# The last layer norm of a decoder step: one engine's work spread over three, the short tile moved up, and the adding transfers reordered

## The chip, the cores and the metric

The kernel runs on one core of a Trainium2 chip. The metric is the device time of one execution in microseconds (us). Three executions of the kernel before took 1103.56, 1101.90 and 1106.04 us; the median is 1103.56 us. The trace that is read here is of one further execution.

## What is computed

The kernel is one inference step of a two-layer decoder trunk for a prompt of 512 tokens and a sample group of 8 tokens, 1024 features each, in float32. Each sub-layer ends in a layer norm. The change concerns only the very last one, the norm behind the mixture of experts of layer 1:

```python
def layer_norm(x, g, b):
    mu = jnp.mean(xf, axis=-1, keepdims=True)
    var = jnp.mean(jnp.square(xf - mu), axis=-1, keepdims=True)
    return ((xf - mu) * lax.rsqrt(var + LN_EPS) * g + b)
...
        xp = layer_norm(ALPHA * xp + hier_moe(xp, ...), ln_g[l, 2], ln_b[l, 2])
        xs = layer_norm(ALPHA * xs + hier_moe(xs, ...), ln_g[l, 2], ln_b[l, 2])
    return (xp, xs, ...)
```

hier_moe gives every token to two experts, its first and its second choice. The token's row of x, already scaled by ALPHA, gets both experts' output rows added, and is then normed and stored.

## The kernel before

The 520 tokens lie in five row tiles, `ROWS = [128, 128, 128, 128, 8]`: tiles 0 to 3 are the prompt, tile 4 is the sample group. `x[:, t, :]` holds a tile, one token per partition, 1024 floats long.

The experts work on sorted blocks of 128 token slots. A block's output goes through ScalarE (L2220) into `ybuf`. All but the last two blocks of layer 1 are written by an indirect transfer from GpSimd's queue (L838) into `y_tok[1]`, a DRAM buffer of 2 x 520 rows: the first half for the tokens' first choices, the second half for the second choices. The last two blocks are held back in SBUF.

The end of the kernel, on each engine:

- GpSimd (POOL) waits until all scattered blocks are in DRAM and then issues ten adding transfers, `add_rows(t, c)` (L871), which read `y_tok` and add onto `x[:, t, :]`; c is the choice. Two adds onto one tile must not overlap, so `add_rows(t, 1)` waits on the queue until `add_rows(t, 0)` has landed (`added[t]`). The order is (0,0) (1,0) (0,1) (2,0) (1,1) (3,0) (2,1) (4,0) (3,1) (4,1). Behind them it loads the count of overflowing blocks, branches past code for such blocks (there are none), and does nothing more.
- TensorE (PE) multiplies the two held blocks by one-hot rows, `held_blocks` (L1666, and L1670 for the short tile), tile by tile, into one of four PSUM pairs, key `("cmb", t)`. A full tile has four matmuls in the code (two blocks, two halves of the row), which the trace records as eight.
- VectorE (DVE), `combine_last`: `summed(t)` waits for both adds of the tile and for its PSUM pair, adds PSUM onto x with the row sum as a by-product (L2773; for tile 4 four pieces at L2778 and a reduce at L2782), and makes minus the mean (L2723). `rooted(t)` waits for ScalarE's square root, takes the reciprocal (L2759), forms (x - mean) * g in place (L2762) and then * scale + b in place (L2763). The order is summed(0), summed(1), rooted(0), summed(2), rooted(1), and so on, so one tile's statistics are taken while the tile before it is finished.
- ScalarE (ACT): `row_squares` sums the squares of x - mean (L1957), a Sqrt activation follows (L2354), and ScalarE's queue issues the stores of the finished tiles (L2348), two tiles behind.

g and b of this norm lie in `lnb[:, 0, :]` and `lnb[:, 1, :]`, one row on every partition. All tiles go in the order 0, 1, 2, 3, 4. xT, which the changed kernel takes as scratch space, has held weights of the last experts' blocks and is read for the last time by the matmuls before `held_blocks`.

Of the kernel before, what the change touches and what calls it, by code (L numbers as in the profile page):

```python
# [27 lines left out]
P = 128  # L28
# [139 lines left out]
def keys(text):  # L168

    return [tuple(int(w) if w.isdigit() else w for w in word.split(".")) for word in text.split()]  # L170
# [67 lines left out]

LATENT_GROUPS = [slice(0, P), slice(P, 2 * P), slice(2 * P, 3 * P), slice(3 * P, 416)]
LATENT_ROWS = {2: [0], 3: [1], 4: [2, 3, 4]}  # L240
COMBINE_DVE = keys("""a.0 b.0 a.1 s.0 b.1 n.0 a.2 s.1 x.0 r.0 b.2 n.1 a.3 s.2 x.1 r.1 b.3 n.2 a.4 s.3 x.2 r.2 b.4 n.3 s.4 x.3 r.3 n.4 x.4 r.4""")


def psum_jobs():

    jobs = []
    jobs += [("xT", -1, t) for t in range(NT)]
    jobs += [("qa", j) for j in range(4)] + [("ka", 0), ("ka", 1), ("va",)]
    jobs += [("kaTok",), ("qr", 0)]
    for step, i in sliding_steps(len(SWA_BLOCKS)):  # L250
        jobs += SWA_WEAVE[i] if step == "W" else [("swa" + step, i)]
    jobs += SWA_SAMPLE
    for n in range(4):
        jobs += [("retS", n), ("retK", n)] + RET_WEAVE.get(("K", n), [])
        jobs += [("retO", n), ("retU", n)] + RET_WEAVE.get(("U", n), [])
        if n:
            jobs += [("retG", n - 1)]
    for l in range(DEPTH):
        if l == 1:
            jobs += LATENT_PE  # L260
            jobs += [("qn", j) for j in (2, 3)]
            jobs += [("qrope", 0)]
            jobs += [("ql", h) for h in range(8)]
            for t in range(NT):
                jobs += ([("qrope", t)] if t else []) + ([("qrT", t - 1)] if t else [])
            jobs += [("qrT", 4)]
            jobs += [("mla" + s, i) for s, i in latent_steps(len(MLA_BLOCKS))]
            jobs += [("pkT", 0), ("pkT", 1), ("pN",)] + [key for key in PAGE_PE if key[0] != "row"]
            jobs += [("uv", j) for j in range(4)]
        jobs += [memory_job(l, *key) for key in MEM_PE[l] if key[0] != "ms2"]  # L270
        if l == 0:
            jobs += [("memF", 1, 0), ("memF", 1, 1), ("rank", 0), ("mkv", 1, 0), ("table", 0), ("mkv", 1, 1)]
        else:
            jobs += [("rank", 1), ("table", 1)]
        for s, b in block_order():
            jobs += [("moe" + s, l, b)] + ([("mkT", 1)] if (l, s, b) == (0, "H", 0) else [])
    jobs += [("cmb", t) for t in range(NT)]
    return jobs


def decoder_step(nc, io, outs):
# [83 lines left out]
    with ExitStack() as ctx:  # L365
# [49 lines left out]
        def part(*dims, at0=None):  # L415
# [7 lines left out]
            if len(dims) > 1:  # L423
# [87 lines left out]
        assert at[0] <= ARENA - EXTRA_SLOTS * PIECE  # L511
        y_front = part(3, 2, D, at0=4096)
        y_of = [y_front[:, t] for t in range(3)] + [pbuf, pT]
        spill_rows, spill_hot = xs[:, 1, :], xsT[:, 1, :, :].rearrange("p k n -> p (k n)")

        at[0] = 0
# [36 lines left out]
                 "var_ready", "rstd_ready", "x_ready", "last_ready", "swapped", "rope_done", "negmax_ready", "probs_ready",  # L553
                 "vec_step", "pool_step", "g_exp", "qd_ready", "vm_ready", "q_state_zero", "q_state_ready", "gated_ready",
                 "row_neg", "row_exp", "row_probs", "router_neg", "router_exp", "moe_exp",
                 "moe_done", "picks_ready", "places_ready", "route_in", "rope_in", "sum_ready", "squares_ready", "lnc_in", "cleared", "held_ready", "root_ready",
                 "wr_zero", "stores_out", "rows_out",
                 "x_out", "x_stored", "half_hidden", "q_wide_zero", "q_wide_ready", "states_out", "tokens_ready", "sq_done", "qrS_zero", "oin_ready", "qrtok_ready"]
        s = {n: sem(n) for n in names}
# [109 lines left out]
        def _(sp):  # L669
# [105 lines left out]
                    expert_rows(0)  # L775
            spilled_weights(1, len(W))


        @block.gpsimd
        def _(pool):  # L780
# [43 lines left out]
            def dispatch(l):  # L824
# [42 lines left out]
                def add_rows(t, c):  # L867
                    first = c * T + t * P
                    if c:
                        pool.wait_ge(added[t], 16)  # L870
                    pool.dma_start(x[0:ROWS[t], t, :], y_tok[1][first:first + ROWS[t], :], accum_op=ALU.add).then_inc(added[t], 16)  # L871

                if l:
                    for i in range(2):
                        pool.wait_ge(y_out[i], 16 * sum(SCATTERED) // 2)
                    add_rows(0, 0)
                    for t in range(NT):
                        if t + 1 < NT:
                            add_rows(t + 1, 0)
                        add_rows(t, 1)  # L880
                sem_ = spill_s[l]
                with spilled(pool, l):
                    full(pool, ("moeX", l, BLOCKS_M - 1))
# [91 lines left out]
            for l in range(DEPTH):  # L975
# [15 lines left out]
                if l == 0:  # L991
                    for t in range(NT):
                        tile_power(t)
                        if t == 3:
                            power(rms[0:P, 0, 2:4])
                    for t in range(1, NT):
                        power(rms[0:ROWS[t], t % 2, 2:4])
                    pool.wait_ge(s["stored"], 16 * n_stored[0])
                    pool.nop().then_inc(s["moe_done"], 1)
            pool.wait_ge(s["stored"], 16 * n_stored[0])  # L1000


        @block.tensor
        def _(pe):
# [649 lines left out]
            def held_blocks():  # L1654

                pe.wait_ge(s["held_ready"], 2)
                for t in range(NT):
                    key = ("cmb", t)
                    o = open_(key)
                    r = ROWS[t]  # L1660
# [260 lines left out]
        def _(act):  # L1921
# [27 lines left out]

            take_xT(-1)  # L1950

            def row_squares(i, t):

                r = ROWS[t]
                act.wait_ge(s["sum_ready"], NT * (i // 3) + t + 1)
                unread = pbuf[0:r, t % 2, :] if i == 3 * DEPTH - 1 else y_of[t][0:r, 0, :]
                act.activation(unread, x[0:r, t, :], ACT.Square, bias=centre[0:r, t % 3:t % 3 + 1],  # L1957
                               accum_out=squares[0:r, t % 3:t % 3 + 1]).then_inc(s["squares_ready"], 1)

            def take_memory(key):  # L1960
                if key[0] == "memF":
# [283 lines left out]
            def latent_attention():  # L2245
# [29 lines left out]
                def turned(i, t):  # L2275
                    take_xT(i, range(t, t + 1))
                    if t + 2 < NT:
                        row_squares(i, t + 2)

                for t in range(2):  # L2280
                    row_squares(2, t)
                steps = {"xT": turned, "oin": latent_squares, "oinT": back,
                         "ukT": lambda: take(("ukT",), ukT, lambda o: o[:, 0:512].rearrange("p (c q) -> p c q", c=4))}
                for key in LATENT_IN:
# [57 lines left out]
            memory_stage(1)  # L2342
            experts(1)

            def store_rows(t):
                act.wait_ge(s["last_ready"], t + 1)
                dst = y_prompt[0, t * P:t * P + P] if t < 4 else y_sample.rearrange("b s d -> (b s) d")
                act.dma_start(dst, x[0:ROWS[t], t, :]).then_inc(s["x_stored"], 16)  # L2348

            for t in range(NT):  # L2350
                row_squares(3 * DEPTH - 1, t)
                r = ROWS[t]
                act.wait_ge(s["squares_ready"], NT + t + 1)
                act.activation(rstd[0:r, t, 0:1], squares[0:r, t % 3:t % 3 + 1], ACT.Sqrt, scale=1.0 / D,  # L2354
                               bias=small[0:r, EPSILON:EPSILON + 1]).then_inc(s["root_ready"], 1)
                if t >= 2:
                    store_rows(t - 2)
            for t in range(NT - 2, NT):
                store_rows(t)
            act.wait_ge(s["x_stored"], 16 * NT)  # L2360


        @block.vector
        def _(dve):
# [354 lines left out]
                dve.wait_ge(y_in[t][0], 16 * (i // 3 + 1))  # L2719
                link(dve.tensor_tensor(x[0:r, t, :], x[0:r, t, :], y_of[t][0:r, 0, :], ALU.add))  # L2720

            def mean_of(i, t, total):
                dve.tensor_scalar(centre[0:ROWS[t], t % 3:t % 3 + 1], total, -1.0 / D, None, ALU.mult).then_inc(s["sum_ready"], 1)  # L2723

            def second_add(i, t):
                r = ROWS[t]
                total = sums[0:r, t % 3:t % 3 + 1]
                dve.wait_ge(y_in[t][1], 16 * (i // 3 + 1))
                link(dve.scalar_tensor_tensor(x[0:r, t, :], y_of[t][0:r, 1, :], 1.0, x[0:r, t, :], ALU.mult, ALU.add, accum_out=total))
                mean_of(i, t, total)  # L2730

            def combine_latents(after):

# [17 lines left out]

            def combine_last():

                def rooted(t):
                    r = ROWS[t]
                    xt = x[0:r, t, :]
                    scale, mid = rstd[0:r, t, 0:1], centre[0:r, t % 3:t % 3 + 1]
                    dve.wait_ge(s["root_ready"], t + 1)
                    link(dve.reciprocal(scale, scale))  # L2759
                    if t == 0:  # L2760
                        dve.wait_ge(s["ln_in"], 32 * 6)
                    link(dve.scalar_tensor_tensor(xt, xt, mid, lnb[0:r, 0, :], ALU.add, ALU.mult))  # L2762
                    dve.scalar_tensor_tensor(xt, xt, scale, lnb[0:r, 1, :], ALU.mult, ALU.add).then_inc(s["last_ready"], 1)  # L2763

                def summed(t):
                    r = ROWS[t]
                    xt = x[0:r, t, :]
                    total = sums[0:r, t % 3:t % 3 + 1]
                    key = ("cmb", t)
                    dve.wait_ge(added[t], 32)  # L2770
                    full(dve, key)
# [3 lines left out]
                    else:  # L2775
# [4 lines left out]
                        free(ins, key)  # L2780
                        taken(dve, key)
                        link(dve.tensor_reduce(total, rowmax[0:r, 0, :], AX.X, ALU.add))  # L2782
                    mean_of(5, t, total)

                summed(0)
                for t in range(NT):
                    if t + 1 < NT:
                        summed(t + 1)
                    rooted(t)

            def first_max(out, m, v, tmp):

# [348 lines left out]
```

## Time and profile before

| | us |
|---|---|
| median of three executions | 1103.56 |
| lowest, highest | 1101.90, 1106.04 |
| span of the profiled execution | 1105.1 |
| TensorE busy | 989.1 |
| VectorE busy | 524.0 |
| ScalarE busy | 353.4 |
| GpSimd busy | 253.4 |

The span is counted from the first instruction, and all times of the trace are positions in it. PE is busy for 90% of it, but not at its end: it does nothing after 1090.1 us, and the last 15 us belong to the other engines and the transfers. A "timeline" lists instructions with their start and length and, in brackets, how long the engine had idled before and what ended that. A "chain" is followed back from the last instruction through whatever released each step. "Windows" give, for a stretch, the busy time of each engine, the granted TensorE clock as a share of full speed, the mean busy share of the 16 DMA engines and the rate in GB/s.

### The profile page before, as it was taken

To read this page: it belongs to the slowest core of one execution; us is meant where nothing else is said; L and a number is where in the kernel's file an instruction comes from. 1 tells how busy PE (TensorE), PEld (TensorE's weight loads), DVE (VectorE), ACT (ScalarE), POOL (GpSimd) and SP (SyncE) were. 2 spreads that over 40 slices of the span, in tenths; PEclk is the share of its full clock that TensorE was granted. 3 is DMA by queue.
4 is the path that set the end of the run, shared out by engine and by line. 5 is a ranking of instruction groups with operands and counts; after the bars stand their busy time and mean duration, and the time that the engine had idled before them with its cause. 6 is when DMAs were issued, how large, how long until landed. Compare 5 with 4: busy or idle time off the path is not lost.

```text
span 1105.1 us, 17827 instructions
## 1 busy us (share of the span) xinstructions
PE 989.1 (90%) x6978; PEld 617.2 (56%) x6978; DVE 524.0 (47%) x1102; ACT 353.4 (32%) x879; POOL 253.4 (23%) x281
## 2 busy tenths in 40 slices
PE   7998999989989998899998398998999946999994
PEld 6886788887446766533332256657568633333331
DVE  0226520566657657143322654773187571334227
ACT  2335531110011523233432342554115422333423
POOL 2224400051500001536311126300000014362121
PEclk9999999998989987899999698899899956999998
DMA  9434702052205407789997404331434063999976
GB/s 313 91 93 114 232 6 77 5 188 77 67 16 179 192 38 300 271 324 410 404 420 273 176 8 101 79 132 40 136 146 185 31 230 102 337 397 405 418 217 161
DMA packets 81594, 204.17 MB, mean 185 GB/s; under 512 B 22682, under 2 KB 47938, under 8 KB 72288
## 3 DMA queue, kind: packets, MB, share of 16 engines
q1 hardware_dynamic: 60976, 151.83, 37.4%
q0 software_dynamic: 19936, 48.99, 14.4%
q10 hardware_dynamic: 592, 2.13, 0.5%
q8 instruction: 59, 0.97, 0.4%
q14 instruction: 31, 0.25, 0.1%
HBM read 184.92 MB, written 25.92 MB: 191 GB/s over the span
## 4 chain that ended last, share of the span: by engine, by line
PE 75%; DVE 13%; DMA 4%; ACT 4%; issue 3%; POOL 0%; SPq 0%; POOLq 0%; DVEq 0%; ACTq 0%
PE PS L1556 15%; PE PS L1393 10%; PE PS L1035 9%; PE PS L1132 6%; PE PS L1571 6%; PE PS L1416 3%; ACT arena L1923 2%; PE PS L1097 2%; DMA x<-y_tok 2%; PE PS L1023 2%; PE PS L1767 2%; PE PS L1058 2%; PE PS L1777 2%; PE PS L1692 2%; PE PS L1545 2%
## 5 line engine op out<-in xcount | busy, mean ns | idle before, releaser
L1923 ACT ACTIVATE arena<-PS 32x520 f32<-32x520 f32 (+10 forms) x150 | 75.1, 513 | 194.2 <-PE PS L1035 47.3
L1556 PE MATMUL PS<-ring,arena 128*32 128x512 f32 x648 | 116.9, 592 | 1.4 <-DVE arena L2934 1.4
L1556 PE MATMUL PS<-arena 128*32 128x512 f32 x648 | 112.8, 614 | 3.5 <-issue 2.6
L1035 PE MATMUL PS<-xT,ring 128*128 128x260 f32 x448 | 102.2, 389 | 4.1 <-DVE arena L2380 3.1
L1035 PEld LDWEIGHTS PS<-xT,ring 128*128 128x128 f32 x448 | 85.5, 192 | 19.8 <-DVE arena L2380 5.1
L2950 DVE COPY arena<-PS 128x256 f32<-128x256 f32 x24 | 10.2, 424 | 171.2 <-PE PS L1564 171.2
L2194 ACT ACTIVATE arena<-PS,lnc 128x128 f32<-128x128 f32 x192 | 69.5, 473 | 42.8 <-PE PS L1545 42.8
L800 POOL TENSOR_TENSOR rstd<-rstd,small 128x1 f32<-128x1 f32 (+1 forms) x25 | 16.3, 651 | 272.7 <-DVE rstd L2668 245.3
L1571 PE MATMUL PS<-ring,arena 128*32 128x512 f32 x432 | 69.0, 595 | 1.2 <-DVE arena L2950 1.2
L1023 PE MATMUL PS<-ident,x 128*128 128x128 f32 (+1 forms) x240 | 39.4, 319 | 33.0 <-DVE x L2744 20.3
L1132 PE MATMUL PS<-ring,xT 128*128 128x256 f32 (+2 forms) x336 | 66.8, 361 | 0.0
L1556 PEld LDWEIGHTS PS<-arena 128*32 128x32 f32 x648 | 30.9, 113 | 62.3 <-issue 58.3
L1132 PEld LDWEIGHTS PS<-ring,xT 128*128 128x128 f32 (+1 forms) x336 | 58.2, 189 | 7.5
L838 POOL DMA_INDIRECT y_tok<-arena,slot_dest x22 | 22.3, 1012 | 174.1 <-ACT arena L2220 168.3
L1023 PEld LDWEIGHTS PS<-ident,x 128*128 128x128 f32 (+1 forms) x240 | 35.1, 202 | 42.0 <-issue 33.2
L1556 PEld LDWEIGHTS PS<-ring,arena 128*32 128x32 f32 x648 | 31.2, 110 | 47.3 <-issue 43.1
L1393 PE MATMUL PS<-ring,xT 128*128 128x512 f32 x128 | 56.8, 593 | 0.7 <-ACT xT L1923 0.7
L1932 ACT ACTIVATE xT<-PS,lnc 128x128 f32<-128x128 f32 (+1 forms) x100 | 37.6, 437 | 54.8 <-PE PS L1023 35.6
L2212 ACT ACTIVATE arena<-PS 128x256 f32<-128x256 f32 x24 | 9.2, 385 | 143.1 <-PE PS L1556 143.1
L1556 PE MATMUL PS<-xT,arena 128*32 128x512 f32 x240 | 50.3, 593 | 0.8 <-DVE arena L2934 0.8
L1393 PE MATMUL PS<-ring,arena 128*128 128x512 f32 x96 | 48.4, 645 | 2.1 <-issue 2.1
L2030 ACT ACTIVATE pbuf<-PS,negmax 128x256 f32<-128x256 f32 (+3 forms) x96 | 45.0, 480 | 10.1 <-DVE negmax L2427 10.0
(422 smaller groups left out, 1858.3 us busy)
## 6 DMA issues: line engine op xcount, KB each, us to landing
arena<-in_moe_w_in_dram SPq DMA_DIRECT2D x27, 1024.0 KB, 10.1
ring<-in_moe_w_in_dram SPq DMA_DIRECT2D x27, 1024.0 KB, 13.5
ring<-in_moe_w_out_dram SPq DMA_DIRECT2D x18, 1024.0 KB, 12.3
ring<-in_w_in_even_dram SPq DMA_DIRECT2D x10, 1024.0 KB, 11.7
xT<-in_moe_w_in_dram SPq DMA_DIRECT2D x10, 1024.0 KB, 13.4
arena<-in_moe_w_out_dram SPq DMA_DIRECT2D x8, 1024.0 KB, 14.5
xT<-in_moe_w_out_dram SPq DMA_DIRECT2D x6, 1024.0 KB, 15.5
y_tok<-in_c_zeros_dram POOLq DMA_DIRECT2D x8, 512.0 KB, 10.2
```

Source lines behind the costliest of these rows:

```text
L838: pool.indirect_dma_start(y_tok[l][:, :], bass.IndirectOffsetOnAxis(ap=slot_dest[:, b:b + 1], axis=0), ybuf[:, buf, :], None, bounds_check ...
L1023: mm = pe.transpose(o[:, chunk_cols(k, r)], by_k[:, k, :], ident[0:r, 0:r])
L1035: mm = pe.matmul(o[out_rows, 512 * h:512 * h + HALF], lhs(k), rhs(k)[:, HALF * h:HALF * h + HALF], start=(k == 0), stop=(k == nk - 1))
L1132: mm = pe.matmul(o[0:ROWS[t], n * width:n * width + width], xT[:, k, tile_cols(t)], w[:, k, cols], start=(k == 0), stop=(k == KD - 1))
L1393: mm = pe.matmul(o[0:ROWS[t], 512 * h:512 * h + 512], out_part(i, 2 * n + k, t), w[:, k, 512 * h:512 * h + 512], start=(n == 0 and k == 0) ...
L1416: mm = pe.matmul(o[:, j * r:j * r + r], w[:, k, j * P:j * P + P], xT[:, k, tile_cols(t)], start=(k == 0), stop=(k == KD - 1))
L1556: mm = pe.matmul(o[group(q), 0:512], xT_[:, k, group(q)], w(q, k), start=(k == 0), stop=(k == KD - 1), **quarter(q))
L1571: mm = pe.matmul(o[group(q), 512 * h:512 * h + 512], a[:, c, group(q)], w(q)[:, c, 512 * h:512 * h + 512], start=(c == 0), stop=(c == 1), ...
L1923: return act.activation(dst, src, ACT.Copy)
L1932: ins = act.activation(dst(k), src(k), ACT.Identity, scale=lnc[:, i, 0, k:k + 1], bias=lnc[:, i, 1, k:k + 1])
L2030: ins = act.activation(prob_view(kind, i)[:, h, :], score_view(kind, i)[:, h, :], ACT.Exp, bias=negmax[:, n % 2, h:h + 1], scale=SCALE[kin ...
L2194: ins = act.activation(dst[:, k, :], o[:, k * P:k * P + P], ACT.Identity, scale=lnc[:, 3 * l + 1, 0, k:k + 1], bias=lnc[:, 3 * l + 1, 1, k ...
```

## The change

The last norm is done in the tile order 0, 4, 1, 2, 3 on all engines. Its element work is split. For each tile VectorE adds PSUM, makes the mean and at once forms (x - mean) * g, not into x but into a scratch row (`centred_rows`, four in xT and one in pT). ScalarE, beside squares and root, multiplies that row by the reciprocal root and writes it to x (`scaled`). GpSimd adds b in place. Only the last tile (3) is finished on VectorE, scale and b in one instruction (`finished`). The stores go from SyncE's queue instead of ScalarE's, one for each tile in the tile order. The ten adding transfers are issued as (0,0) (4,0) (1,0) (2,0) (0,1) (4,1) (3,0) (1,1) (2,1) (3,1).

```diff
+LAST_TILES = [0, 4, 1, 2, 3]
+LAST_ADDS = [(0, 0), (4, 0), (1, 0), (2, 0), (0, 1), (4, 1), (3, 0), (1, 1), (2, 1), (3, 1)]
...
-    jobs += [("cmb", t) for t in range(NT)]
+    jobs += [("cmb", t) for t in LAST_TILES]
...
+        centred_rows = [xT[:, :, :].rearrange("p k n -> p (k n)")[:, D * i:D * i + D] for i in range(4)] + [pT[:, 0, :]]
...
+            for n, t in enumerate(LAST_TILES):
+
+                if n < NT - 1:
+                    sp.wait_ge(s["last_ready"], n + 1)
+                else:
+                    sp.wait_ge(s["end_ready"], 1)
+                dst = y_prompt[0, t * P:t * P + P] if t < 4 else y_sample.rearrange("b s d -> (b s) d")
+                sp.dma_start(dst, x[0:ROWS[t], t, :]).then_inc(s["x_stored"], 16)
...
-                    add_rows(0, 0)
-                    for t in range(NT):
-                        if t + 1 < NT:
-                            add_rows(t + 1, 0)
-                        add_rows(t, 1)
+                    for t, c in LAST_ADDS:
+                        add_rows(t, c)
...
+            pool.wait_ge(s["ln_in"], 32 * 6)
+            for n, t in enumerate(LAST_TILES[:-1]):
+
+                r = ROWS[t]
+                pool.wait_ge(s["scaled_ready"], n + 1)
+                pool.tensor_tensor(x[0:r, t, :], x[0:r, t, :], lnb[0:r, 1, :], ALU.add).then_inc(s["last_ready"], 1)
...
-                for t in range(NT):
+                for t in LAST_TILES:
                     key = ("cmb", t)
...
+            def scaled(n):
+
+                t = LAST_TILES[n]
                 r = ROWS[t]
-                act.wait_ge(s["squares_ready"], NT + t + 1)
-                act.activation(rstd[0:r, t, 0:1], squares[0:r, t % 3:t % 3 + 1], ACT.Sqrt, scale=1.0 / D,
+                act.wait_ge(s["centred_ready"], n + 1)
+                act.wait_ge(s["inverse_ready"], n + 1)
+                act.activation(x[0:r, t, :], centred_rows[n][0:r, :], ACT.Copy, scale=rstd[0:r, t, 0:1]).then_inc(s["scaled_ready"], 1)
+
+            for n, t in enumerate(LAST_TILES):
+                row_squares(3 * DEPTH - 1, n, t)
+                r = ROWS[t]
+                act.wait_ge(s["squares_ready"], NT + n + 1)
+                act.activation(rstd[0:r, t, 0:1], squares[0:r, n % 3:n % 3 + 1], ACT.Sqrt, scale=1.0 / D,
                                bias=small[0:r, EPSILON:EPSILON + 1]).then_inc(s["root_ready"], 1)
-                if t >= 2:
-                    store_rows(t - 2)
-            for t in range(NT - 2, NT):
-                store_rows(t)
-            act.wait_ge(s["x_stored"], 16 * NT)
+                if n:
+                    scaled(n - 1)
...
+                def finished(n, t):
+
+                    r = ROWS[t]
+                    dve.wait_ge(s["inverse_ready"], NT)
+                    dve.wait_ge(s["centred_ready"], NT)
+                    dve.scalar_tensor_tensor(x[0:r, t, :], centred_rows[n][0:r, :], rstd[0:r, t, 0:1], lnb[0:r, 1, :], ALU.mult, ALU.add
+                                             ).then_inc(s["end_ready"], 1)
...
+                    mean_of(n, t, total)
+                    dve.wait_ge(s["sum_ready"], NT + n + 1)
+                    if n == 0:
+                        dve.wait_ge(s["ln_in"], 32 * 6)
+                    dve.scalar_tensor_tensor(centred_rows[n][0:r, :], xt, centre[0:r, n % 3:n % 3 + 1], lnb[0:r, 0, :], ALU.add, ALU.mult
+                                             ).then_inc(s["centred_ready"], 1)
+
+                for n, t in enumerate(LAST_TILES):
+                    summed(n, t)
+                    if n:
+                        rooted(n - 1, LAST_TILES[n - 1])
+                rooted(NT - 1, LAST_TILES[-1])
+                finished(NT - 1, LAST_TILES[-1])
```

`rooted(n, t)` now holds only the wait for the root and the reciprocal. n is the position in the order, t the tile.

## Rows read from the trace of the kernel before

**Rows 1.** Chain of waits towards the end: start us, us, what.

```profile
1064.87 5.49 DMA x<-y_tok
...
1071.28 8.46 DMA x<-y_tok
...
1080.02 7.22 DMA x<-y_tok
```

**Rows 2.** Windows: us, each engine's busy time, TensorE clock, DMA share, GB/s.

```profile
1073.00:1085.00 12.00, 12.00 (x43) 4.93 (x36) 3.99 (x8) 5.14 (x7) 3.46 (x4) 1.00 1.05 202
...
1101.00:1102.00 1.00, 0.00 (x0) 0.00 (x0) 0.96 (x2) 0.00 (x0) 0.00 (x0) 0.50 0.96 389
```

**Rows 3.** Timeline of VectorE, the tail: start us, us, engine, line, tiles, shapes.

```profile
1078.89 1.23 DVE L2773 SCALAR_TENSOR_TENSOR x<-PS,x 128x1024 f32<-128x1024 f32 x1 [7.53 <-PE PS L1666]
...
1087.26 1.23 DVE L2773 SCALAR_TENSOR_TENSOR x<-PS,x 128x1024 f32<-128x1024 f32 x1 [0.80 <-DMA x<-y_tok]
...
1088.53 0.15 DVE L2723 TENSOR_SCALAR bns<-bns 128x1 f32<-128x1 f32 x1
...
1088.79 1.29 DVE L2762 SCALAR_TENSOR_TENSOR x<-x,bns,lnb 128x1024 f32<-128x1024 f32 x1
...
1091.31 1.22 DVE L2773 SCALAR_TENSOR_TENSOR x<-PS,x 128x1024 f32<-128x1024 f32 x1
...
1095.36 0.41 DVE L2778 SCALAR_TENSOR_TENSOR x<-PS,x 8x256 f32<-8x256 f32 x1
...
1097.31 0.14 DVE L2723 TENSOR_SCALAR bns<-bns 8x1 f32<-8x1 f32 x1
...
1101.56 1.27 DVE L2763 SCALAR_TENSOR_TENSOR x<-x,rstd,lnb 8x1024 f32<-8x1024 f32 x1
```

**Rows 4.** TensorE's lines of the held blocks: ns min/median/max, first and last start.

```profile
L1666 PE MATMUL PS<-arena x32: 590/592/697, 1075.1 to 1088.5; 128*128 128x512 f32 x32
...
L1670 PE MATMUL PS<-arena x16: 377/379/383, 1089.0 to 1089.7; 128*8 128x256 f32 x16
```

**Rows 5.** Timeline and one line of ScalarE, the tail, with its stores.

```profile
1075.26 1.11 ACT L2220 ACTIVATE arena<-PS,arena 128x1024 f32<-128x1024 f32 x1 [3.50 <-PE PS L1571]
...
1088.72 1.15 ACT L1957 ACTIVATE pbuf<-x,bns 128x1024 f32<-128x1024 f32 x1 [3.37 <-DVE bns L2723]
...
1089.99 0.29 ACT L2354 ACTIVATE rstd<-bns,small 128x1 f32<-128x1 f32 x1
...
L2348 ACTq DMA_DIRECT2D out_dram<-x x5: 338/339/540, 1090.0 to 1102.9; - x5
```

**Rows 6.** GpSimd's additions of b in earlier norms, by line: ns min/median/max.

```profile
L816 POOL TENSOR_TENSOR x<-x,lnb x10: 2360/2372/2380, 468.8 to 993.5; 128x1024 f32<-128x1024 f32 x8, 8x1024 f32<-8x1024 f32 x2
```

**Rows 7.** Timeline near 982 us, and the same VectorE line over the whole span.

```profile
982.41 2.37 POOL L816 TENSOR_TENSOR x<-x,lnb 128x1024 f32<-128x1024 f32 x1
982.62 2.31 DVE L2931 TENSOR_SCALAR arena<-arena 128x256 f32<-128x256 f32 x1
...
L2931 DVE TENSOR_SCALAR arena<-arena x24: 282/286/2307, 470.7 to 1066.7; 128x256 f32<-128x256 f32 x24
```

**Rows 8.** Timeline from 281 us: VectorE beside four additions of GpSimd.

```profile
281.30 8.05 POOL L961 TENSOR_TENSOR arena<-arena,small 8x1024 f32<-8x1024 f32 x4
281.99 1.47 DVE L2395 TENSOR_TENSOR arena<-xT,arena 8x256 f32<-8x256 f32 x1
...
287.17 0.41 DVE L2395 TENSOR_TENSOR arena<-xT,arena 8x256 f32<-8x256 f32 x1
287.62 1.22 DVE L2659 SCALAR_TENSOR_TENSOR x<-x,PS 128x1024 f32<-128x1024 f32 x1
```

**Rows 9.** Timeline near 619 us, and GpSimd's line L800 over the whole span.

```profile
618.87 1.22 DVE L2729 SCALAR_TENSOR_TENSOR x<-arena,x 128x1024 f32<-128x1024 f32 x1
619.04 1.48 POOL L800 TENSOR_TENSOR rstd<-rstd,small 128x1 f32<-128x1 f32 x1 [10.81 <-DVE rstd L2739]
...
L800 POOL TENSOR_TENSOR rstd<-rstd,small x25: 536/550/1480, 290.7 to 889.8; 128x1 f32<-128x1 f32 x20, 8x1 f32<-8x1 f32 x5
```

## What the change is expected to do

> **What bounds the kernel now.** I read the chain of waits towards the end first, then the tail's timeline engine by engine, then the windows. Up to 1087 us the chain runs through the adding transfers: the one at 1064.87 lands 5.49 us later, at 1070.36, that at 1071.28 lands at 1079.74, that at 1080.02 at 1087.24 [rows 1]. Between 1073 and 1085 us the DMA engines are at a share of 1.05 and move 202 GB/s [rows 2], so a 512 KB add costs 2.5 us of them, and TensorE is busy throughout the same 12 us. VectorE waits for TensorE before tile 0 (at 1078.89) and for a transfer before tile 2 (1087.26, after only 0.80 us idle) [rows 3]. From there it never waits: tile 2 to tile 3 takes 1091.31 - 1087.26 = 4.05 us, and its last instruction ends at 1101.56 + 1.27 = 1102.8 [rows 3]. The last store is issued at 1102.9 [rows 5]; the span is 1105.1. So the end belongs to VectorE from 1087 us, to transfers and TensorE before. TensorE's last matmul of the held blocks starts at 1089.7 [rows 4], so tile 3 can't be combined before 1090.1 whatever else is done.
>
> **The adds in another order.** The bytes are the same, 8 x 512 KB and 2 x 32 KB. Now four adds without a wait among them stand in the queue, and (0,1), (4,1), (3,0), (1,1) follow while data still flows. Each waits for a first add that was issued three or more places earlier, so I expect no gap in the flow. Tile 4's two adds are early; tile 3's second is last. But (0,1), third in the queue before, now stands behind (2,0): it takes the place of the fourth large transfer, which landed at 1079.74 [rows 1]. Tile 0 therefore starts between 1078.9 (TensorE, as before [rows 3]) and 1079.9; I take 1079.3, 0.4 later than before. The other tiles follow at 2.5 us each: tile 1 after about 84.4, tile 2 after 86.9, tile 3 after 89.4 at the latest (1000 left out here and below). VectorE comes later than that to each of them (below). On TensorE the short tile's matmuls move from the end to second place, a microsecond, and tile 3's end stays at 90.1.
>
> **VectorE.** A full tile is now the add (1.27 us to the mean), 0.19 from the mean to the next dependent instruction (that is what ScalarE's start at 88.72 is behind 88.53 [rows 3, 5]), one long instruction instead of two, 1.25 (the two before took 91.31 - 88.79 = 2.52), and 0.07 for the reciprocal's issue (88.79 - 88.53 less 0.19): 2.78 us in place of 4.05 [rows 3]. The short tile takes 97.31 - 95.36 = 1.95 for its pieces, so 3.46. Undisturbed: tile 0 at 79.3, short tile at 82.0, reciprocal of tile 0 at 85.4, tile 1 at 85.47, its centred product 86.93 to 88.2.
>
> **ScalarE.** Squares to root is 89.99 - 88.72 = 1.27, the root 0.29; the scaling is one ACTIVATE, 1.11 for the same form at L2220 and 1.15 at L1957 [rows 5]; I take 1.13. Together 2.7 us in each 2.78: it fits, and the load of the root's table lies where it lay.
>
> **GpSimd.** It adds b to four tiles, the short one at full price since the free length counts: 2.37 us each, from ten instructions between 2.36 and 2.38 [rows 6], 9.5 us in all against 7 us taken off VectorE at 1.28 a piece. It is free for this from about 85 us, behind its last transfer.
>
> **The shared resource.** Alone GpSimd would keep pace. But the rows show that it and VectorE exclude each other. A VectorE TENSOR_SCALAR that takes 0.29 us took 2.31 when GpSimd's L816 had begun 0.21 before it, and ended 0.15 after GpSimd (982.62 + 2.31 against 982.41 + 2.37) [rows 7]. A TENSOR_TENSOR with both inputs in SBUF took 1.47 in place of 0.41 beside GpSimd's L961; beside the same line an add of PSUM and SBUF took its usual 1.22 [rows 8]. The other way round GpSimd's power took 1.48 instead of 0.55 when VectorE's SCALAR_TENSOR_TENSOR of two SBUF rows had begun first [rows 9]. The new centred product (x and g) and `finished` (centred row and b) both have two SBUF inputs; the PSUM add doesn't. The Trainium skill, "SBUF — State Buffer", section "Who interferes with whom", states it as a rule: VectorE with two SBUF inputs and a GpSimd instruction that reads SBUF use one read port, whoever issues first holds it for the whole instruction. By that rule the end is the one forecast here; if it did not hold for these forms, the first rival's.
>
> **The sum.** From 88.2, when tile 1's centred product ends, the port is never free, as each side has its next piece ready before the other ends (VectorE's next product is ready 1.5 us after it gets free, GpSimd holds 2.37; ScalarE delivers within 1.4): add to tile 0, centred 2, add to tile 4, centred 3, add to tile 1, `finished` on tile 3, add to tile 2. That is 4 x 2.37 + 3 x 1.25 = 13.2, so GpSimd ends at 101.4. Then both tile 2's and tile 3's stores leave SyncE, in that order. The old last store (32 KB) took 1105.1 - 1102.9 = 2.2 from issue to the end [rows 5]; at 389 GB/s [rows 2] each 512 KB adds 1.35. End: 101.4 + 0.05 + 2.2 + 2.7 = 1106.3 against 1105.1 of the profiled execution: +1.2 us. That a store leaves from SyncE and not from ScalarE I cost at nothing (-0.3 to +0.5; nothing is queued before it there). The profiled execution lies 1.5 above the median of 1103.56, so the forecast is 1103.56 + 1.2 = 1104.8. With tile 0 between 78.9 and 79.9 and the port's handover up to 0.15 each time, this case alone gives 1103.3 to 1106.3.
>
> **First rival, the port does not bind** (or only partly). The SCALAR_TENSOR_TENSOR of 128x1024 has no row where it waited for GpSimd, only one where GpSimd waited for it. Then VectorE reaches tile 3 at 91.0, its mean at 92.3, root at 94.05, `finished` ends at 95.6; ScalarE has scaled tile 2 at 95.2, GpSimd ends at 97.65, the end is 102.6: -2.5 us, 1101.1. This is the most the split can give, since tile 2's b and two large stores still follow. Chance 0.22.
>
> **Second rival, slower: GpSimd gets the port first each time.** The reciprocal of the tile before starts two races. ScalarE starts 0.19 after it, takes 1.13, GpSimd follows by 0.1: 1.42. VectorE: 0.07 + 1.27 + 0.19 = 1.53, then wants the port. At tile 1 ScalarE is still held by the short tile's root, so that GpSimd comes about even, at 86.8 to 87.0 against 86.93. If GpSimd wins there, VectorE's product waits 2.37, the next reciprocal with it, and the race starts again with the same lead of 0.1: a cycle of 2.37 + 1.25 + 0.19 + 1.13 + 0.1 = 5.0 us. The fourth add starts at 86.8 + 15.1 = 101.9, ends at 104.3, the run at 109.2: +4.2, 1107.7. It decides from a lead of some 0.1 us. For it: the lead. Against: GpSimd's instruction may need the port only some time after its recorded start. Chance 0.27. Past 0.5% it goes only if each cycle is 0.35 longer still.
>
> **Third, the queued adds come out worse**: with (0,1) one transfer later (at 81.8) all shifts by 2.5, to 1107.3. Chance 0.06.
>
> **The numbers.** 0.5%, 5.5 us, is about what a measurement of this kernel tells from no change. Likeliest case 0.41; first rival 0.22, second 0.27, third 0.06; 0.04 for something outside the tail. Nearly all lie within 5.5 us. A gain above that would need an end at 1099.6, before what the first rival reaches, so 0.07, most of it from scatter in the medians (4 us between lowest and highest); slower by more 0.09, from the second rival with longer cycles; same 0.84. Range 1100.0 to 1108.6: it takes in the first two rivals.
>
> **What would show it.** Right: four GpSimd additions from 88 us, each beginning where a long VectorE instruction ends, recorded lengths above 2.37; VectorE's centred products of tiles 2 and 3 and `finished` stretched by 0.8 to 2.3; the last landing add near 89; two stores issued together at about 101.4. First rival: all VectorE instructions at 1.28. Second: the products of tiles 1, 2 and 3 all at 3.5 us, a 5.0 us cycle. The forecast is wrong from its start if tile 0 begins outside 78.9 to 79.9.

## Result, and the profile after

| | before | changed |
|---|---|---|
| median, first measurement | 1103.62 us | 1113.86 us |
| ratio, with 95% interval | | 1.0100 (1.0073 to 1.0127) |
| ratio, measured again | | 1.0086 (1.0061 to 1.0111) |
| span of the profiled execution | 1105.1 | 1116.2 |
| PE, DVE, ACT, POOL busy | | 985.8, 525.4, 357.4, 262.1 |
| from the first adding transfer to the end | 40.2, 39.9, 39.9 | 47.6, 48.9, 47.7 |

The changed kernel is slower by some 10 us. A span is about 2 us shorter than the device time of the same execution: the traced execution of the changed kernel took 1118.29 us, the longest of its four, and its span is 1116.2. The last row is what I work with from here and call the tail, from GpSimd's first adding transfer to the end of the span. With that transfer the change begins to act, and what lies ahead of it scatters by several us from one execution to the next. Three traces of each kernel give 40.0 and 48.0 us on average: 8.0 of the 9.4 to 10.2 us between the medians lie in the tail.

The chain of waits of the changed kernel, towards the end (start us, us, what); it answers to [rows 1]:

```profile
1068.66 5.40 DMA x<-y_tok
...
1074.57 8.32 DMA x<-y_tok
...
1098.86 1.16 ACT x L2367
1100.01 0.07 issue
1100.08 2.34 POOL x L1015
1102.42 2.44 issue
1104.86 0.04 POOLq L367
1104.90 2.33 POOL x L1015
```

The chain ends with GpSimd's last addition, and that ends at 1107.2, nine us ahead of the end of the span. VectorE's timeline, against [rows 3]:

```profile
1082.91 1.22 DVE L2792 SCALAR_TENSOR_TENSOR x<-PS,x 128x1024 f32<-128x1024 f32 x1 [7.76 <-DMA x<-y_tok]
...
1084.37 1.28 DVE L2806 SCALAR_TENSOR_TENSOR xT<-x,bns,lnb 128x1024 f32<-128x1024 f32 x1
...
1089.08 1.22 DVE L2792 SCALAR_TENSOR_TENSOR x<-PS,x 128x1024 f32<-128x1024 f32 x1
...
1090.53 3.35 DVE L2806 SCALAR_TENSOR_TENSOR xT<-x,bns,lnb 128x1024 f32<-128x1024 f32 x1
1093.80 0.14 DVE L2774 RECIPROCAL rstd<-rstd 8x1 f32<-8x1 f32 x1
1093.88 1.19 DVE L2792 SCALAR_TENSOR_TENSOR x<-PS,x 128x1024 f32<-128x1024 f32 x1
...
1095.30 3.39 DVE L2806 SCALAR_TENSOR_TENSOR xT<-x,bns,lnb 128x1024 f32<-128x1024 f32 x1
...
1098.69 1.20 DVE L2792 SCALAR_TENSOR_TENSOR x<-PS,x 128x1024 f32<-128x1024 f32 x1
...
1100.12 3.39 DVE L2806 SCALAR_TENSOR_TENSOR pT<-x,bns,lnb 128x1024 f32<-128x1024 f32 x1
```

and ScalarE's scalings and GpSimd's additions beside it:

```profile
1089.17 1.13 ACT L2367 ACTIVATE x<-xT,rstd 128x1024 f32<-128x1024 f32 x1
...
1094.04 1.15 ACT L2367 ACTIVATE x<-xT,rstd 8x1024 f32<-8x1024 f32 x1 [1.94 <-DVE rstd L2774]
```

```profile
1090.45 2.34 POOL L1015 TENSOR_TENSOR x<-x,lnb 128x1024 f32<-128x1024 f32 x1 [3.56 <-ACT x L2367]
1095.27 2.33 POOL L1015 TENSOR_TENSOR x<-x,lnb 8x1024 f32<-8x1024 f32 x1 [2.48 <-ACT x L2367]
1100.08 2.34 POOL L1015 TENSOR_TENSOR x<-x,lnb 128x1024 f32<-128x1024 f32 x1 [2.48 <-ACT x L2367]
1104.90 2.34 POOL L1015 TENSOR_TENSOR x<-x,lnb 128x1024 f32<-128x1024 f32 x1 [2.48 <-ACT x L2367]
```

Read the two side by side. GpSimd starts at 1090.45, 1095.27, 1100.08; VectorE's products start at 1090.53, 1095.30, 1100.12, each a few hundredths later, and take 3.35 to 3.39 us instead of the 1.28 of the first one (1084.37), beside which GpSimd does nothing. None of the additions is stretched. Up to GpSimd's last addition this is the second rival of the prediction: a cycle of 4.82 us where it had 5.0.

The queue instructions that close the program, changed kernel (ns min/median/max, first and last start):

```profile
L367 POOLq DRAIN  x1: 10973/10973/10973, 1105.0 to 1105.0; - x1
L367 SPq COMPARE_BRANCH  x1: 38/38/38, 1111.2 to 1111.2; - x1
...
L367 POOLq EVENT_SEMAPHORE  x2: 17/17/17, 1116.0 to 1116.1; - x2
```

and of the kernel before:

```profile
L365 POOLq COMPARE_BRANCH  x1: 38/38/38, 1089.3 to 1089.3; - x1
L365 POOLq DRAIN  x1: 8732/8732/8732, 1089.5 to 1089.5; - x1
...
L365 ACTq COMPARE_BRANCH  x1: 38/38/38, 1104.7 to 1104.7; - x1
```

SyncE passes its wait for the stores at 1111.2. The run goes on to 1116.2 because GpSimd's DRAIN does: it starts in the queue at 1105.0, while the last addition still works, and ends at 1105.0 + 10.97 = 1116.0, which is 8.76 us behind that addition's end. Before, the same DRAIN ran from 1089.5 to 1098.2, under VectorE's work, and the end was the stores' (1104.7).

### The profile page after: what moved, and what is told of

It reads as the page before. It is cut to its first block, busy times and chain, and to the rows that moved or that the text cites. A ratio compares the mean times of both kernels' runs of the same rounds, so it can differ in the third digit from the quotient of the medians.

```text
span 1116.2 us, 17837 instructions
## 1 busy us (share of the span) xinstructions
PE 985.8 (88%) x6978; PEld 613.1 (55%) x6978; DVE 525.4 (47%) x1098; ACT 357.4 (32%) x883; POOL 262.1 (23%) x285
## 4 chain that ended last, share of the span: by engine, by line
PE 72%; DVE 12%; DMA 6%; ACT 4%; issue 4%; POOL 1%; SPq 0%; POOLq 0%; DVEq 0%; ACTq 0%
PE PS L1572 14%; PE PS L1409 10%; PE PS L1051 8%; PE PS L1148 6%; PE PS L1587 5%; PE PS L1432 3%; ACT arena L1939 2%; PE PS L1113 2%; PE PS L1783 2%; PE PS L1039 2%; PE PS L1708 2%; DMA arena<-in_moe_w_in_dram 2%; PE PS L1074 2%; PE PS L1793 2%; PE PS L1561 1%
## 5 line engine op out<-in xcount | busy, mean ns | idle before, releaser
L2975 DVE COPY arena<-PS 128x256 f32<-128x256 f32 x24 | 10.2, 424 | 175.1 <-PE PS L1580 175.1
## 6 DMA issues: line engine op xcount, KB each, us to landing
y_tok<-in_c_zeros_dram POOLq DMA_DIRECT2D x8, 512.0 KB, 10.2
```

## Experiments

All ratios are to the kernel before on the same chip. Tails: as defined above.

| kernel | ratio (95%) | tail us |
|---|---|---|
| e1, split undone | 0.9981 (0.9961 to 1.0002) | 38.9 |
| e2, before with a late GpSimd instruction | 1.0064 (1.0044 to 1.0083) | 47.2 |
| e3, VectorE first at the port | 1.0033 (1.0018 to 1.0049) | 44.8 |
| e4, products with one SBUF input | 1.0010 (0.9983 to 1.0036) | 41.5 |
| r5, changed again | 1.0086 (1.0061 to 1.0111) | 48.9 |
| r6, split undone, short tile first | 0.9976 (0.9959 to 0.9994) | 36.9 |
| r7, GpSimd adds b to two tiles | 1.0034 (1.0011 to 1.0056) | 40.0 |
| r8, r6 with the last tile in halves | 0.9965 (0.9946 to 0.9984) | 36.6 |

**e1: the order without the split.** VectorE finishes each tile behind its reciprocal; `scaled` and GpSimd's loop are gone.

```diff
-                    dve.reciprocal(scale, scale).then_inc(s["inverse_ready"], 1)
+                    link(dve.reciprocal(scale, scale))
+                    dve.scalar_tensor_tensor(x[0:r, t, :], centred_rows[n][0:r, :], scale, lnb[0:r, 1, :], ALU.mult, ALU.add
+                                             ).then_inc(s["last_ready"], 1)
```

> The changed kernel with the split undone: tile order, order of the adds, scratch rows and SyncE's stores stay, but VectorE finishes every tile itself (product with g, then scale and b), ScalarE does squares and root only and GpSimd nothing behind its last transfer. Theory (exclusion on VectorE's and GpSimd's shared port, and the 8.7 us DRAIN that closes GpSimd's program, now starting behind its last addition): both are gone; VectorE needs 4 x 4.05 + 4.7 = 20.9 us from 79.3, ends at 100.2, a 512 KB store follows: about 1 us below the kernel before (-3 to +1), 11 below the changed one. Rival (the new order of the adds, the stores from SyncE or something ahead of the tail costs the 10 us): stays 3 to 10 us above the kernel before.

Measured: ratio 0.9981, tail 38.9, 1.1 under the kernel before. Its closing rows:

```profile
L367 POOLq DRAIN  x1: 10458/10458/10458, 1081.1 to 1081.1; - x1
L367 SPq COMPARE_BRANCH  x1: 38/38/38, 1099.6 to 1099.6; - x1
```

GpSimd is through at 1091.6, the stores at 1099.6. The times alone don't tell this kernel from the one before (the interval takes in 1). So the tile order, the reordered adds and SyncE's stores together cost nothing that shows, and the whole loss is the split's.

**e2: the DRAIN alone.** The kernel before, with this ahead of GpSimd's last wait:

```diff
+            pool.wait_ge(s["last_ready"], NT)
+            pool.memset(wr[:, 0, 0, 20:21], 0.0)
```

> The kernel before with one addition: behind the last norm GpSimd clears one column of a tile that nobody reads any more (0.1 us of work). Theory of the DRAIN: the 8.73 us that it took from 1089.5 start anew behind the last GpSimd instruction, at about 1102.9, so the run ends at 1111.6: +6.5 us. Rival (the DRAIN only waits for something else, transfers or the other engines): no change, within 1 us.

Measured: ratio 1.0064, tail 47.2, 7.2 us more (6.5 expected) for 0.1 us of work. The instruction in the timeline, and the closing rows:

```profile
1096.82 0.10 POOL L1001 MEMSET wr<- 128x1 f32 x1 [14.41 <-DVE x L2765]
```

```profile
L365 POOLq DRAIN  x1: 8732/8732/8732, 1097.0 to 1097.0; - x1
L365 ACTq COMPARE_BRANCH  x1: 38/38/38, 1098.6 to 1098.6; - x1
```

The stores are in at 1098.6, the DRAIN ends at 1105.7, the span at 1105.9. So the DRAIN, begun in the kernel before 13 us ahead of the last VectorE instruction's end and here 0.2 us behind it, takes the same 8.73 us: it doesn't wait for the other engines, nor for the stores. It isn't always 8.73, though. In e1, r6 and r8, where GpSimd's last work is an adding transfer, as in the kernel before, it took 10.46, 9.22 and 9.21 us; what it does in that time no run shows.

**e3: VectorE first at the port.** The call of `rooted(n - 1, ...)` moves from behind the product to between the PSUM add and `mean_of`.

> The changed kernel with each reciprocal moved behind the next tile's PSUM add, so that ScalarE's scaling and GpSimd's addition start 1.3 us later and VectorE's product gets the port first. Theory of the port: the cycle falls from 4.81 us to 1.25 + 2.37 = 3.62, the products are stretched by under 1 us, GpSimd ends some 3.6 us earlier and the run with it: 3.6 below the changed kernel, still 5 to 7 above the one before since the DRAIN follows. Rival (the cycle is set by the chain of semaphores through three engines, not by the port): a later reciprocal only makes it longer, +1 us or more against the changed kernel.

Measured: ratio 1.0033, tail 44.8, 3.3 under the changed kernel's average. GpSimd's additions and two of VectorE's products:

```profile
1083.65 2.35 POOL L1015 TENSOR_TENSOR x<-x,lnb 128x1024 f32<-128x1024 f32 x1 [4.03 <-ACT x L2367]
1086.39 2.90 POOL L1015 TENSOR_TENSOR x<-x,lnb 8x1024 f32<-8x1024 f32 x1 [0.39 <-ACT x L2367]
1091.20 2.35 POOL L1015 TENSOR_TENSOR x<-x,lnb 128x1024 f32<-128x1024 f32 x1 [1.91 <-ACT x L2367]
```

```profile
1083.70 3.39 DVE L2808 SCALAR_TENSOR_TENSOR xT<-x,bns,lnb 128x1024 f32<-128x1024 f32 x1
...
1088.51 1.86 DVE L2808 SCALAR_TENSOR_TENSOR xT<-x,bns,lnb 128x1024 f32<-128x1024 f32 x1
```

A later reciprocal made the kernel faster, so a chain of semaphores is not what sets the cycle. But the edit didn't do what it was meant to: GpSimd won the first grant all the same (1083.65 against 1083.70). The second addition came while that product held the port, and took 2.90; it ended at 1089.29 and the next product, waiting since 1088.51, ended 1.08 behind it. Both directions of the exclusion stand in these five rows. The four additions start 2.74, 4.81 and 3.28 us apart (the last at 1094.48), 10.8 us in all where I had expected 3 x 3.62 = 10.9 and the changed kernel has 14.4. That the sum fits is luck, as the turns at the port weren't the ones that I had forecast.

**e4: one SBUF input.** The products read the tile's PSUM pair in place of g and, for tile 3, b, so the last norm's g, and b of tile 3, are left out.

```diff
-                    dve.scalar_tensor_tensor(centred_rows[n][0:r, :], xt, centre[0:r, n % 3:n % 3 + 1], lnb[0:r, 0, :], ALU.add, ALU.mult
-                                             ).then_inc(s["centred_ready"], 1)
+                    free(dve.scalar_tensor_tensor(centred_rows[n][0:r, :], xt, centre[0:r, n % 3:n % 3 + 1], pair(key)[0:r, :], ALU.add, ALU.mult
+                                             ), key)
```

> The changed kernel, but VectorE's long products read the tile's PSUM pair where they read g and b (so g of the last norm is left out, and b of tile 3, and PSUM values stand in their place). They have one SBUF input only. Theory of the port: every product takes 1.2 to 1.3 us, the cycle is 2.8 us, GpSimd's last addition ends 7 us earlier than in the changed kernel, and the end, still its end plus 8.7 us of DRAIN, 6 to 7 us earlier: 2 to 4 us above the kernel before. Rival (any VectorE instruction is held while GpSimd works, or the chain of semaphores sets the cycle): products at 3.4 us and a cycle of 4.8 as in the changed kernel.

Measured: ratio 1.0010, tail 41.5, 6.5 under the changed kernel's average. The products' line and the fourth product, three of the additions, and SyncE's closing row:

```profile
L2804 DVE SCALAR_TENSOR_TENSOR xT<-x,bns,PS x4: 1269/1280/1281, 1078.2 to 1087.1; 128x1024 f32<-128x1024 f32 x3, 8x1024 f32<-8x1024 f32 x1
...
1089.82 1.28 DVE L2804 SCALAR_TENSOR_TENSOR pT<-x,bns,PS 128x1024 f32<-128x1024 f32 x1
```

```profile
1084.25 2.36 POOL L1015 TENSOR_TENSOR x<-x,lnb 128x1024 f32<-128x1024 f32 x1 [3.84 <-ACT x L2367]
1086.87 2.34 POOL L1015 TENSOR_TENSOR x<-x,lnb 8x1024 f32<-8x1024 f32 x1 [0.27 <-ACT x L2367]
1089.80 2.36 POOL L1015 TENSOR_TENSOR x<-x,lnb 128x1024 f32<-128x1024 f32 x1 [0.58 <-ACT x L2367]
```

```profile
L367 SPq COMPARE_BRANCH  x1: 37/37/37, 1098.8 to 1098.8; - x1
```

The same instruction over the same number of elements, beside the same additions, takes 1.28 instead of 3.39 once one of its inputs lies in PSUM. The product at 1089.82 has the very tie of the changed kernel, a few hundredths behind an addition's start (1089.80), and isn't held. That is the port shown on the form that the change uses. The Trainium skill, "SBUF — State Buffer", section "Who interferes with whom", states the rule for two SBUF inputs, and these traces agree with it.

The stores are in at 1098.8 here, 36.5 us into the tail, and the run ends 5.0 us later with the DRAIN. Without it e4 would end 0.4 us behind its stores, as e1 does, with a tail of 36.9 (an estimate from these two traces), 2.0 below e1's 38.9. So where nothing is held at the port the split would shorten the end, and the DRAIN takes more than it gives.

**r5 and r11: the changed kernel again; r9 and r10: the one before.**

> The changed kernel once more, beside the next ones. Its first measurement was 10.3 us above the kernel before; from GpSimd's first adding transfer to the end its trace takes 47.6 us against 40.2, which accounts for 7.4. Theory (the tail is all of it): ratio about 1.0067, tail of 47.6 again. Rival (something ahead of the tail costs 3 us more): ratio 1.009 to 1.010 again.

> The kernel before, unchanged, traced again. The medians put the changed kernel 9.4 to 10.3 us higher, the tails (from GpSimd's first adding transfer to the end) 7.4 to 8.7. Theory (the tail is all of it and the traced tail of 40.2 us is a long one among its executions): a tail of 38 to 39.5. Rival (the rest lies ahead of the tail): 40.2 again within 0.3, and the first adding transfer earlier than the changed kernel's by 1.5 to 3 us on average.

> The same once more, for the scatter of tail and of what lies ahead: as in the run before it.

> The changed kernel, unchanged, traced a third time on the same chip. Theory: a tail between 47.4 and 49, GpSimd first in each of the races, its last addition followed by 8.76 us and nothing else. Rival (the port's first grant differs from one execution to the next): a tail near 45, with GpSimd's first addition behind VectorE's product.

Measured: tails 48.9 and 47.7, 39.9 and 39.9. In r5 and r11 GpSimd again starts ahead of all three products, by 0.03 to 0.07 us; the grant did not vary. The extra us in r5's tail is the transfer (0,1), which took 9.54 us to land against 8.32; r5's ratio of 1.0086 lies between the theory's and the rival's. The theory of r9, a long traced tail, failed: 39.9 and not 38 to 39.5. Its rival, a cost ahead of the tail, fits only in part: first adding transfers lie at 1064.9, 1062.2, 1063.6 before and at 1068.7, 1064.4, 1067.5 in the changed kernel, 3.3 later on average, but at 1061.1, 1062.3 and 1063.7 in e3, e4 and r7, which share its code up to there. Where the remaining 1.4 to 2.2 us between the medians come from stays open.

**r7: GpSimd only while it is early.** It adds b for tiles 0 and 4; the other three are finished on VectorE.

```diff
-            for n, t in enumerate(LAST_TILES[:-1]):
+            for n, t in enumerate(LAST_TILES[:2]):
...
+                    if n > 2:
+                        finished(n - 1, LAST_TILES[n - 1])
```

> The changed kernel, but GpSimd adds b only for the first two tiles of the order (0 and 4); VectorE finishes the other three. Theory: tiles 1 and 2 still have their products held for 2.1 us each, but GpSimd is done 29 us into the tail, so its DRAIN (8.7 us) ends before the stores do and costs nothing; VectorE ends 36.7 us into the tail, the end is at 40.4: level with the kernel before, 7 us under the changed one. Rival (the DRAIN follows the last engine to finish, or the port's cycle alone is the loss): a tail above 44.

Measured: tail 40.0, where 40.4 was expected. Its closing rows:

```profile
L367 POOLq DRAIN  x1: 10977/10977/10977, 1090.6 to 1090.6; - x1
...
L367 SPq COMPARE_BRANCH  x1: 37/37/37, 1103.4 to 1103.4; - x1
```

The DRAIN ends at 1101.5, under the stores. The ratio is 1.0034 though, above 1 with its whole interval, where the expectation was level with the kernel before: its ten times fall into two groups, 1101.3 to 1106.0 and 1108.7 to 1111.8, and the trace is of the first. What the second group does wasn't traced, so the miss in the times is unexplained.

**r6: short tile first.** e1, with

```diff
-LAST_TILES = [0, 4, 1, 2, 3]
-LAST_ADDS = [(0, 0), (4, 0), (1, 0), (2, 0), (0, 1), (4, 1), (3, 0), (1, 1), (2, 1), (3, 1)]
+LAST_TILES = [4, 0, 1, 2, 3]
+LAST_ADDS = [(4, 0), (0, 0), (1, 0), (4, 1), (0, 1), (2, 0), (1, 1), (3, 0), (2, 1), (3, 1)]
```

> The kernel with the order alone (split undone), and the order now 4, 0, 1, 2, 3 with the adds (4,0) (0,0) (1,0) (4,1) (0,1) (2,0) (1,1) (3,0) (2,1) (3,1). VectorE had idled 8.3 us before tile 0; the short tile's 4.7 us of work go there. Theory (VectorE's work from tile 0 on sets the end): tile 0 starts 15.1 us behind the first adding transfer, when TensorE has it, four tiles at 4.05 and a last root and product of 1.4 give 32.7, the store 3.1: a tail of 35.8 us against 38.9 with the order 0, 4, 1, 2, 3 and 40.2 before: ratio 0.996. Rival (transfers bind all along, each tile waits for its adds): a tail of 38 to 40 and waits on transfers before tiles 2 and 3.

Measured: ratio 0.9976, tail 36.9, 3.1 under the kernel before but 1.1 above the 35.8 expected. TensorE, VectorE:

```profile
1077.95 0.62 PE L1677 MATMUL PS<-arena 128*8 128x256 f32 x8 [0.85 <-ACT arena L2227]
```

```profile
1078.71 0.41 DVE L2788 SCALAR_TENSOR_TENSOR x<-PS,x 8x256 f32<-8x256 f32 x1 [5.83 <-PE PS L1677]
...
1082.32 1.22 DVE L2783 SCALAR_TENSOR_TENSOR x<-PS,x 128x1024 f32<-128x1024 f32 x1 [0.19 <-PE PS L1673]
...
1090.65 1.22 DVE L2783 SCALAR_TENSOR_TENSOR x<-PS,x 128x1024 f32<-128x1024 f32 x1 [0.18 <-DMA x<-y_tok]
```

The miss: the last held block reaches SBUF late (ScalarE, L2227), and the short tile's eight matmuls of the first block cover less of that than a full tile's do. TensorE idles 0.85 us, so tile 0 starts 15.9 into the tail instead of 15.1; before tile 2 a transfer adds 0.18.

**r8: the last tile in two halves.** r6, the closing product of tile 3 over two column halves with a store each.

> As the kernel with the short tile first, and the last tile's closing product is made and stored in two halves of 512 columns. Theory: the first half is stored while VectorE makes the second, and the second store is half as long: 0.6 us less, a tail of 35.2 us. Rival: the second store's fixed time hides it, no difference within 0.3 us.

Measured: ratio 0.9965, tail 36.6: 0.3 less than r6, half of what I expected, and at the bound that I gave the rival. Of the 0.3, 0.18 is r6's wait for a transfer before tile 2, which r8's trace doesn't have; the tails of the kernel before differ by 0.3 among themselves, and the intervals of r6 and r8 overlap. So a gain from the halves isn't shown. r8 is faster than the kernel before by 0.35% and than the changed one by 1.2%.

## Why the prediction was wrong

**The end of GpSimd's program had no term.** The sum let the run end with the stores. With 8.76 us of DRAIN behind GpSimd's last addition, and 0.24 from there to the end of the span, even the forecast's own case gives 101.4 + 8.76 + 0.24 = 1110.4 instead of 1106.3: +5.3 us, and the first rival 1106.6. That is the larger part of the miss: +5.3 in place of +1.2, with a measured +7.4 in the first trace's tail (47.6 against 40.2). The instruction was there in the trace of before, in the closing rows shown above. I looked only at work that was on the path, and a DRAIN that ends at 1098.2 under VectorE is on no path. The step "it is free for this from about 85 us" asked when GpSimd could begin and not what follows when it ends.

**The turns at the port were the other way round.** The exclusion was right in kind ([rows 7] to [rows 9] hold for the new form), and the cycle of the second rival was sized well: 5.0 us against 4.82. Its fourth addition ends 38.6 us into the tail (1107.24 - 1068.66), where the likeliest case had 101.4 - 64.87 = 36.5: 2.1 us more, and with the 5.3 from the DRAIN that is the measured 7.4. I had given the tie at tile 1 to VectorE on two grounds, and both fell. ScalarE was barely held by the short tile's root: the scaling began 0.27 behind the reciprocal's start (1089.17), against 0.24 and 0.25 in the next two cycles. And GpSimd needed no lead worth the name: it recorded a start 0.03 to 0.08 us ahead in twelve such ties of five traces and had the port each time. The sum of the second rival itself had the lead of 0.1 right.

**The transfers came out as forecast.** The second add of tile 0 landed 82.89 - 68.66 = 14.2 us into the tail (14.4 in the sum) in the first trace; in r5 it was 15.5, half a us past the bound that the prediction set for tile 0. The second adds of tiles 2 and 3 landed about a us later than in the sum, but tiles 1 to 3 never waited for one. The windows show the DMA engines at 205 GB/s from 1072 to 1091 without a gap, against 202 in [rows 2]:

```profile
1072.00:1091.00 19.00, 18.39 (x100) 7.13 (x93) 9.57 (x24) 8.09 (x11) 6.06 (x8) 1.00 1.06 205
```

**The stores were priced too high.** I gave the last pair 4.95 us from GpSimd's last addition to the end. In the changed kernel that addition ends at 1107.24 and SyncE is past its wait at 1111.2; with 0.4 us from there to the end, as in e1 (1099.6 to 1100.0), that is 4.4. I had added two whole transfers to the 2.2 us of a small one; which part of the 2.2 was too much isn't shown. One reading was wrong besides, without effect: the 1105.1 that I set beside the median of 1103.56 is a span, and a span is about 2 us shorter than a device time, so the traced execution lay further above the median than 1.5. The forecast used only the difference of two spans.

**Put together**, from e1's tail of 38.9: the port holds the three products 2.1 us each, and GpSimd's additions end behind VectorE's last product, so that the stores would let the run end at 1111.2 + 0.4 = 1111.6, 43.0 us into the tail; the DRAIN adds 4.6, to 47.6. The split alone costs 8.7 us between these two traces. It saves nothing here, for of the 5.1 us that leave VectorE (1.28 on each of four tiles) 6.3 come back as waiting.

## What to carry to other kernels

Before giving the last work of a kernel to an engine, look in the closing rows at what that engine still does behind its last instruction: here GpSimd's DRAIN takes 8.7 us and more, so its last instruction has to end some 9 us ahead of the kernel's end. Before work goes to GpSimd to relieve VectorE, count the SBUF inputs of VectorE's instructions in that stretch: with two, the engines took turns and VectorE waited longer than it had been relieved; with one (e4) nothing was held. No split measured here ended below the kernel without one (e1): e4 was kept above it by the DRAIN, and r7, with GpSimd early, had 40.0 against 38.9. Moving the small tile into an idle stretch, without splitting anything (r6), was worth 2.0 us more than e1's order.

## What the runs showed that I had not expected

- GpSimd's closing DRAIN: 8.73 us in e2 and in the kernel before; 8.76 to 8.77 from the end of the last addition or clearing to the DRAIN's end in e2, e3, e4, r5, r7, r11 and the changed kernel; 9.2 to 10.5 in e1, r6 and r8.
- GpSimd got the port with a recorded lead of a few hundredths of a us: 0.05 in e3, 0.03 in the changed kernel's second cycle, and it held the port for its full 2.34 us each time. No trace has VectorE ahead by as little, so it isn't shown whether the earlier start decides such a tie or GpSimd wins it anyway; a product that had the port since 1086.0 kept it against an addition that came at 1086.39 (e3).
- A 128x1024 SCALAR_TENSOR_TENSOR with two SBUF inputs that was held ended 1.08 to 1.09 us behind GpSimd's addition, of 1.28 alone: at most 0.2 us of its work was done before the release, however long it had waited.
